# Hymba decode step with PEER retrieval on one core: tiles 4+5, 6+7 and 8+sample share one pass over w_out and w_query

## The reference

```python
h = rmsnorm(x, g_mix) ; c_q, c_kv, k_r, r_q, r_k, r_v, r_g = split(h @ w_in)   # (1024, 2464)
lat = mla_attend(...)                 # 8 heads, latent width 128, causal
ro  = retention(...)                  # 8 heads of 64x64 state, chunks of 128, a scan
x = x + concat(lat @ w_uv, head_norm(ro) * silu(r_g)) @ w_out      # w_out (1024, 1024)
h = rmsnorm(x, g_ffn)
q = h @ w_query                       # w_query (1024, 1024)
for each token and each of 8 heads:   # product keys: 2 x 128 scores, top 16 of each,
    e, gate = top 16 of the pair sums # then top 16 of their sums -> 16 experts
x = x + sum over 128 experts of gate * gelu(u_experts[e] . h) * v_experts[e]
y = rmsnorm(x, g_final)
```

## Time and profile before

| | |
|---|---|
| median of three runs | 3395.66 us (3386.74 to 3405.19) |
| the profiled execution | 3404.81 us, its span 3403.0 us |
| granted TensorE clock | 0.946 of full speed |
| DMA | 1298.59 MB, mean 382 GB/s |
| busy share of TensorE, VectorE, ScalarE, POOL | 86%, 68%, 46%, 38% |

### The profile page before, as it was taken

How to read it: one execution, slowest core, us unless ns; L and a number is a source line. 1 busy time by engine, 2 the same in 40 slices (tenths; PEclk the granted TensorE clock), 3 DMA queues, 4 the chain that set the end, 5 groups by cost and what they waited for, 6 DMA issues and landing times.

```text
span 3403.0 us, 32496 instructions
## 1 busy us (share of the span) xinstructions
PE 2916.1 (86%) x9486; PEld 1498.2 (44%) x9486; DVE 2321.7 (68%) x5531; ACT 1550.6 (46%) x4211; POOL 1300.5 (38%) x1097
## 2 busy tenths in 40 slices
PE   7989899988889898989899878987898888787777
PEld 5755555543445444544444333533353344443222
DVE  1268738785687658774788578866876587677854
ACT  2147334554356344643456345644563455333333
POOL 0023324443344433343445434443444434343432
PEclk8998999999999999999999999999999999899899
DMA  4289999999999999999999999999999999799998
GB/s 173 90 318 362 385 384 405 392 406 418 417 392 388 422 422 408 392 399 417 421 396 414 422 421 422 405 421 422 400 373 418 422 353 330 299 373 421 372 422 346
DMA packets 238361, 1298.59 MB, mean 382 GB/s; under 512 B 45748, under 2 KB 70228, under 8 KB 95462
## 3 DMA queue, kind: packets, MB, share of 16 engines
q0 software_dynamic: 156672, 1140.92, 82.3%
q1 hardware_dynamic: 81510, 155.59, 12.2%
HBM read 1279.41 MB, written 16.44 MB: 381 GB/s over the span
## 4 chain that ended last, share of the span: by engine, by line
PE 44%; DMA 27%; DVE 21%; ACT 4%; issue 2%; POOL 0%; SPq 0%; DVEq 0%; ACTq 0%; POOLq 0%
PE PS L1080 21%; DMA R<-in_t_uv,idx 19%; DVE R L1728 8%; PE PS L763 8%; DMA R<-in_t_uv,idxS 4%; DMA wring<-in_w_out 2%; PE PS L844 2%; PE PS L1002 2%; PE PS L729 2%; PE PS L843 2%; DVE SC L1689 2%; DVE SC L1686 2%; DVE ef L1691 2%; DMA wring<-in_w_query 2%; PE PS L1029 2%
## 5 line engine op out<-in xcount | busy, mean ns | idle before, releaser
L1080 PE MATMUL PS<-R,diag 128*128 128x512 f32 x3616 | 1788.4, 630 | 295.8 <-ACT diag L1355 262.8
L694 POOL DMA_INDIRECT R<-in_t_uv,idx x1024 | 1236.6, 1208 | 1981.1 <-PE PS L1080 1236.6
L1728 DVE CUSTOM_DVE_ANT_0 R<-R,hb 128x1024 f32<-128x1024 f32 x1088 | 1316.3, 1219 | 663.0 <-DMA R<-in_t_uv,idx 581.8
L1080 PEld LDWEIGHTS PS<-R,diag 128*128 128x128 f32 x3616 | 672.1, 198 | 1172.3 <-issue 606.9
L1346 ACT ACTIVATE acts<-dots 128x1 f32<-128x1 f32 x1088 | 217.8, 200 | 1258.8 <-DVE dots L1728 1256.2
L1355 ACT ACTIVATE diag<-ident,wv 128x128 f32<-128x128 f32 x840 | 337.7, 402 | 46.3 <-PE PS L1080 19.3
L763 PE MATMUL PS<-R 128*128 128x256 f32 (+1 forms) x1280 | 296.1, 388 | 42.6 <-ACT stg L1123 36.4
L1348 ACT ACTIVATE wv<-gate,acts 128x1 f32<-128x1 f32 x1024 | 302.0, 295 | 33.2
L763 PEld LDWEIGHTS PS<-R 128*128 128x128 f32 x1280 | 245.9, 199 | 111.8 <-issue 80.2
L1739 DVE SCALAR_TENSOR_TENSOR xb<-R,wv,xb 128x1024 f32<-128x1024 f32 x184 | 235.7, 1281 | 9.5 <-ACT wv L1348 9.5
L1466 DVE CUSTOM_DVE_ANT_0 PP<-PS,mask 128x144 f32<-128x144 f32 (+7 forms) x64 | 49.4, 771 | 170.8 <-PE PS L844 170.7
(11 more groups left out here) (242 smaller groups left out, 2389.9 us busy)
## 6 DMA issues: line engine op xcount, KB each, us to landing
wring<-in_w_out SPq DMA_DIRECT2D x64, 512.0 KB, 12.0
wring<-in_w_query SPq DMA_DIRECT2D x64, 512.0 KB, 8.3
R<-in_t_win SPq DMA_DIRECT2D x27, 1024.0 KB, 12.0
R<-in_t_uv,idx POOLq DMA_INDIRECT x1024, 12.6
pr<-prd SPq DMA_DIRECT2D x8, 976.0 KB, 11.2
prd<-stg SPq DMA_DIRECT2D x54, 128.0 KB, 7.6
xb<-in_x_prompt SPq DMA_DIRECT2D x8, 512.0 KB, 8.5
R<-in_w_out SPq DMA_DIRECT2D x8, 512.0 KB, 4.7
```

The source lines that it names most:

```text
L694: e.indirect_dma_start(dst, None, table, bass.IndirectOffsetOnAxis(ap=index, axis=0)).then_inc(S[s], c.count(name, s, 16))
L1080: m = mm(bank(n), diag[:, NTH[s] % DR, :], pair(s)[:, D + 512 * n:D + 512 * n + 512], start=begins, stop=s == last_slot(t), skip_group_che ...
L1728: e.tensor_tensor_reduce(u, u, hb[:, tile_of(g) % 2, :], 1.0, 0.0, ALU.mult, ALU.add, dots[:, g % NW:g % NW + 1]).then_inc(dve_done, c.cou ...
```

## The change

Tiles 4 and 5, 6 and 7, 8 and 9 become pairs (`PAIRED`), a first tile a and a second tile b. One pass over w_out and one over w_query serves both: `pout`, `pnorm` and `pquery` (34 parts, 48 turns) take the place of two tails, and each block in the ring is used by four matmuls (`pair_rows`, banks 2, 3 for a and 5, 6 for b). The ring of such a pass has two buffers; the third (`spare`) holds a's concatenated heads, then b's normalised input, then b's transposed queries. b's residual x2 lives in `pr`; x2 and h of b are stored to DRAM (`kept`) and loaded into `xb` and `hb` when b's turn comes. b's scores are made later (`scb`). The attention of b, and before it `kv` and `q`, stand ahead of the pair's pass. The sample's loads, attention and retention stand 128 turns earlier. The third pass of `items` ends at turn 464, not 540. The ring of gathers is wide for slots 472 to 671 instead of 550 to 775. Tiles 1 to 3 keep tails of their own, with fewer turns for tile 3.

```diff
@@ -40,7 +40,8 @@
 NR = AUX + 7
 DR = 4
 NW = 16
-WIDE = 4 * P + 38, 6 * P + 8
+WIDE = 3 * P + 88, 5 * P + 32
+PAIRED = {4: 5, 6: 7, 8: SMP}
+    both = lambda a: stage("pout", a) + stage("pnorm", a) + stage("pquery", a)
+    for n, at, end in ((1, 8, 160), (2, 182, 3 * P + 80)):
         spread(stage("ldx", n), at, at + 1)
         spread(prep(n), at + 8, at + 22)
         spread(stage("ldw", n), at + 22, at + 23)
         spread(stage("items", n), at + 26, end)
-    for t in range(1, NTILE):
-        at = P * (t - 1)
-        if t > 1:
-            spread(top(t, 1), at, at + 40)
-        spread(stage("att", t + 1) + stage("ret", t + 1), at + (3 if t > 1 else 17), at + (52 if t > 1 else 58))
-        spread(stage("ldb", t + 1), at + 36 if t > 1 else 8, at + 37)
-        spread(tail(t + 1), at + (52 if t > 1 else 58), at + 96)
-        spread(top(t + 1, 0), at + 96, at + 119)
-        if t + 2 <= NTILE:
-            spread(stage("lda", t + 2), at + 56, at + 57)
-            spread(stage("kv", t + 2) + stage("q", t + 2), at + 100, at + 128)
-    at = P * (NTILE - 2)
-    spread(stage("ldc", SMP), at + 18, at + 52)
-    spread(stage("lds", SMP), at + 54, at + 60)
-    spread(stage("kv", SMP) + stage("q", SMP), at + 97, at + 108)
-    spread(stage("atts", SMP) + stage("rets", SMP), at + 108, at + 180)
-    at += P
-    spread(top(NTILE, 1), at, at + 40)
-    spread(tail(SMP), at + 52, at + 82)
-    spread(top(SMP, 0) + top(SMP, 1), at + 82, at + 118)
-    spread(stage("sts", SMP), at + 84, at + 116)
+    for t in range(2, NTILE + 1):
+        spread(top(t, 1), P * (t - 1), P * (t - 1) + 40)
+    spread(stage("att", 2) + stage("ret", 2), 17, 58)
+    spread(stage("ldb", 2), 8, 9)
+    spread(tail(2), 58, 96)
+    spread(top(2, 0), 96, 119)
+    spread(stage("lda", 3), 56, 57)
+    spread(stage("kv", 3) + stage("q", 3), 100, 126)
+    spread(stage("att", 3) + stage("ret", 3), P + 3, P + 48)
+    spread(stage("ldb", 3), P + 34, P + 35)
+    spread(tail(3), P + 48, P + 86)
+    spread(top(3, 0), P + 92, P + 118)
+    spread(stage("lda", 4), P + 52, P + 53)
+    spread(stage("ldb", 4), P + 60, P + 61)
+    spread(stage("kv", 4) + stage("q", 4), P + 86, P + 98)
+    spread(stage("att", 4) + stage("ret", 4), P + 98, 2 * P + 8)
+    spread(stage("lda", 5) + stage("ldb", 5), 2 * P + 8, 2 * P + 10)
+    spread(stage("kv", 5) + stage("q", 5), 2 * P + 10, 2 * P + 18)
+    spread(stage("att", 5) + stage("ret", 5), 2 * P + 18, 2 * P + 52)
+    for a in PAIRED:
+        at = P * (a - 3)
+        if a > 4:
+            spread(stage("scb", a - 1), at + 41, at + 43)
+            spread(stage("att", a) + stage("ret", a), at + 43, at + (100 if a < NTILE else 94))
+            spread(stage("ldb", a), at + 84, at + 85)
+            spread(top(a - 1, 0), at + 94, at + 119)
+            if a < NTILE:
+                spread(stage("lda", a + 1) + stage("ldb", a + 1), at + 100, at + 102)
+                spread(stage("kv", a + 1) + stage("q", a + 1), at + 108, at + 128)
+                spread(stage("att", a + 1) + stage("ret", a + 1), at + P + 3, at + P + 50)
+        spread(both(a), at + P + 52, at + P + 100)
+        spread(top(a, 0), at + P + 100, at + P + 120)
+        if a < NTILE:
+            spread(stage("lda", a + 2), at + P + 102, at + P + 103)
+            spread(stage("kv", a + 2) + stage("q", a + 2), at + P + 108, at + P + 128)
+    at = P * (NTILE - 3)
+    spread(stage("ldc", SMP), at + 48, at + 82)
+    spread(stage("lds", SMP), at + 94, at + 98)
+    spread(stage("kv", SMP) + stage("q", SMP), at + 100, at + 110)
+    spread(stage("atts", SMP) + stage("rets", SMP), at + 110, at + 180)
+    spread(stage("sts", SMP), at + P + 58, at + P + 90)
+    at = P * (NTILE - 1)
+    spread(stage("scb", SMP), at + 41, at + 43)
+    spread(top(SMP, 0) + top(SMP, 1), at + 43, at + 118)
...
-        gfin = wring[:, 2, :]
+        gfin = wring[:, 0, :]
+        spare = wring[:, 2, :]
+        xpr, tpr = pr[:, 0:D], pr[:, D:2 * D]
+
+        def cat_of(t):
+            return spare if t in PAIRED else hb[:, (t + 1) % 2 if is_b(t) else t % 2, :]
+
+        def kept_of(t, what):
+            row = P * (2 * (t - 1) + what)
+            return kept[row:row + P, :]
+
+        def before(t):
+            return t - 3 if is_b(t) else t - 2
...
-            return 4 if t == 1 else 3
+            return 4 if t == 1 else 2 if t in PAIRED else 3
 
         def w_buf(t, m):
-            return R[:, m % 4, :] if t == 1 else wring[:, m % 3, :]
+            return R[:, m % 4, :] if t == 1 else wring[:, m % w_bufs(t), :]
...
-                e.wait_ge(dve_done, c.at("dve", f"ret{t - 1}"))
+                if is_b(t - 1):
+                    e.wait_ge(pe_done, c.at("pe", f"qqT{t - 1}"))
+                else:
+                    e.wait_ge(dve_done, c.at("dve", f"ret{t - 1}"))
...
+            def load_gfin(t):
+                e.wait_ge(pe_done, c.at("pe", f"used q{t}_{NCH - 1}"))
                 dma(gfin, A["g_final"].partition_broadcast(P), "gfin", f"g{t}")
+
+            def pout(p, a):
+                b = PAIRED[a]
+                yield from p.to(0)
+                for m in range(2):
+                    load_w(a, m, p)
+                e.wait_ge(dve_done, c.at("dve", f"s sn{DEC_B - 1}" if b == SMP else f"ret{b}"))
+                if b == SMP:
+                    x = A["x_sample"].rearrange("b t d -> (b t) d")
+                    dma(xpr[0:NSMP, :], x, "xp", f"a{b}")
+                    dma(xpr[NSMP:P, :], x, "xp", f"x{b}")
+                else:
+                    dma(xpr, x_rows[P * (b - 1):P * b, :], "xp", f"x{b}")
+                for m in range(2, NCH + 2):
+                    yield from p.to(5 + m - 2)
+                    load_w(a, m, p)
+
+            def pnorm(p, a):
+                b = PAIRED[a]
+                yield from p.to(0)
+                e.wait_ge(dve_done, c.at("dve", f"res{b}"))
+                dma(kept_of(b, 0), xpr, "x2st", f"x{b}")
+                yield from p.to(2)
+                e.wait_ge(dve_done, c.at("dve", f"hp{b}"))
+                dma(kept_of(b, 1), spare, "hst", f"h{b}")
+
+            def pquery(p, a):
+                for m in range(NCH + 2, 2 * NCH):
+                    yield from p.to(1 + m - 2 - NCH)
+                    load_w(a, m, p)
+                yield from p.to(8)
+                load_gfin(a)
...
-                if t == SMP:
-                    dma(xb[0:NSMP, t % 2, :], A["x_sample"].rearrange("b t d -> (b t) d"), f"xb{t % 2}", f"a{t}")
-                    dma(xb[NSMP:P, t % 2, :], A["x_sample"].rearrange("b t d -> (b t) d"), f"xb{t % 2}", f"x{t}")
+                if is_b(t):
+                    e.wait_ge(S["x2st"], c.at("x2st", f"x{t}"))
+                    dma(xb[:, t % 2, :], kept_of(t, 0), f"xb{t % 2}", f"x{t}")
+                    e.wait_ge(S["hst"], c.at("hst", f"h{t}"))
+                    dma(hb[:, t % 2, :], kept_of(t, 1), "hbl", f"h{t}")
...
+                for k in range(NCH):
+                    yield from p.to(4 + k)
+                    if k == 0:
+                        e.wait_ge(act_done, c.at("act", f"catT{b}"))
+                    pair_rows(a, k, k, "o")
+
+            def pair_rows(a, m, k, which):
+                e.wait_ge(S[f"w{m % 2}"], c.at(f"w{m % 2}", f"{which}{a}_{k}"))
+                w = w_buf(a, m)
+                for lhs, at in ((T1, 2), (tpr, 5)):
+                    for n in range(2):
+                        i = mm(bank(at + n), lhs[:, P * k:P * k + P], w[:, 512 * n:512 * n + 512],
+                               start=k == 0, stop=k == NCH - 1)
+                i.then_inc(pe_done, c.count(f"used {which}{a}_{k}"))
...
+            def pquery(p, a):
+                b = PAIRED[a]
+                for k in range(NCH):
+                    yield from p.to(k)
+                    if k == 0:
+                        e.wait_ge(act_done, c.at("act", f"hT{b}"))
+                    pair_rows(a, k + NCH, k, "q")
+                yield from p.to(9)
+                e.wait_ge(act_done, c.at("act", f"qq{b}"))
+                transposes(lambda k: scr[:, P * k:P * k + P], H,
+                           lambda k: two(5)[:, P * k:P * k + P]).then_inc(pe_done, c.count(f"qqT{a}"))
+                yield from p.to(11)
+                e.wait_ge(act_done, c.at("act", f"qqT{a}"))
+                scores(a, B1)
+                yield from p.to(13)
+                e.wait_ge(act_done, c.at("act", f"sc{a}"))
+                transposes(lambda k: xpr[:, P * k:P * k + P], H,
+                           lambda k: two(5)[:, P * k:P * k + P]).then_inc(pe_done, c.count(f"qqT{b}"))
+
+            def scb(p, b):
+                yield from p.to(0)
+                e.wait_ge(act_done, c.at("act", f"qqT{b}"))
+                if b < SMP:
+                    e.wait_ge(act_done, c.at("act", f"qlat{b + 1}"))
+                scores(b, spare)
```

187 lines of the change are left out of this document (145 added, 42 removed).

## The result

The changed kernel takes 3441.65 us (median of 4 runs, 3434.39 to 3446.47) against 3392.51 us for the kernel before (4 runs, 3386.74 to 3405.19). The ratio on record is 1.0123 [1.0098, 1.0148]: it is slower, by some 42 us.

The account below looks back on a forecast made before the run. Bytes set the time nearly everywhere, TensorE and chains between engines limiting attention. Terms -49 +60 +5 +18 -5 -5 gave +24 us on 3404.8 us, 3429 us, or 3420 us on the medians' scale; range 3360 to 3475 us.

Parts of the forecast that it names:

- The bytes: Whole kernel: net 20.5 MB less to move, entered as -49 us wherever the DMA is full.
- The main term: Slots 226 to 356: 412 us of matmul take 457 us against 388 us of bytes, 10 absorbed; +60 us.
- absorption: Slots 226 to 356: the gather ring of 8 buffers takes up about 10 us of slower consumption.
- packing share: Slots 226 to 356: how full TensorE can be, 0.89 in the first 82 slots, 0.95 in the pair's 48.
- The ring of two: Pairs' tails: two weight buffers lose 21 us per pair unabsorbed; entered as +5 us second pair, +18 us third.
- the short ring: Rival, 12%: slow weight loads cost 32 us more per pair, 3516 us; sign: waits of 2 us or more per block.
- Stretches after the pairs: After each pair slots should run at 2.5 us each; slots 868 to 1014 at a DMA share of 1.0.
- The sample's attention: Moved 128 slots earlier beside a list search, it keeps its length in slots and costs the same: 0.
- The rival that the bytes decide: Rival, 25% with its neighbourhood: gather ring absorbs every TensorE wait; 3342 to 3371 us, slots 226 to 356 under 395 us.
- Balance: Rival, 22%: TensorE packs at 0.95 and the third pair's loss is partly absorbed; -15 us, 3390 us.

Follow-up runs that it names:

- Experiment 1: Kernel before, loading half the columns of each w_out and w_query block from tile 4 on: 3354.14 us, ratio 0.987.
- x3_half_items: Changed kernel with every second row block left out of the input projection's third pass: 3425.05 us, ratio 1.0077.
- z4_after_dve: Changed kernel with 19 more slots in 226 to 259 and 316 to 355 summed by VectorE instead of TensorE: 3430.1 us, ratio 1.0082.
- y1_att8_dense: Kernel before with the attention and retention of tile 8 in 34 slots instead of 49: 3411.17 us, ratio 1.005.
- y3_pairs45_67: Changed kernel without its third pair, tile 8 and the sample tailed apart and their stages where they stood before: 3442.29 us, ratio 1.0133.

## Why the prediction was right, and where it was off

**The bytes.** "Net 20.5 MB less" was exact: 20.45 MB. Their worth, "-49 us, wherever the DMA is full", was mis-sized. Experiment 1 gives 36 us (27 to 45) for as many, and its tails by the traces 40. Why a MB gives back less than its rate is not shown: the tails of before stand at a DMA share of 1.01 to 1.02. This is the term of the sum that the runs correct. With -36 in its place the sum is +37 us, and the runs' difference is 42. That they come so close is partly luck, as neither is known to better than some 10 us.

**The main term.** "+60 us" for slots 226 to 356. The stretch took 437 us where I had 457, or 447 after absorption, with TensorE busy 410.2 us (my sum was 412 us) and 155.0 MB (mine 157.5):

```profile
911.00:1348.00 437.00, 202.35 (x426) 77.16 (x424) 0.98 0.91 355
...
911.00:1348.00 437.00, 57.91 (x248) 47.96 (x249) 0.98 0.91 355
...
DMA packets 25440, 155.00 MB, mean 355 GB/s; under 512 B 3105, under 2 KB 5285, under 8 KB 8357
```

The first of these rows is the value matmuls alone (mine 204 us), the second the items of the input projection (mine 49 us). Packing was 0.94 over the whole stretch, better than my 0.90 (412 of 457 us). As a loss beyond the bytes, which is how the +60 was defined, it is 437 less 155.0 MB at 406 GB/s (382 us), 55 us before anything that the ring absorbs; the slot times cannot show whether the 10 us of absorption were there. The term was right within some 10 us, and what it gave too much, the stretches behind it gave back too little (-14 where I had -24), which fits bytes worth less.

**What sets the pace there.** The prediction spoke of TensorE's sum over a packing share. The runs show that over 130 slots this is only part. Taking 17 and 24 us from TensorE (x3_half_items, z4_after_dve) shortened the stretch by 7 us each time. One reason is that the sum binds in shorter pieces: in the dense attention of y1_att8_dense, which cost 17 us, TensorE is busy 112.8 of 116 us, and z4_after_dve relieved a pass that was then near the time of its bytes. The other is a cost that TensorE's sum does not hold: smaller lumps returned 13 us and the third buffer 14 us with the same matmuls. A likely link is order: each engine takes its parts in a fixed order, and with fewer slots between a head's parts VectorE and ScalarE stand before its mask and exponent while the slots' own work is queued behind. That chain is in the timeline of one head; that it accounts for the rest in numbers is argued, not shown.

**The ring of two.** "21 us are lost per pair where nothing absorbs them", entered as 5 and 18: a third buffer returned 14 us in all, and in the third pair ring, lumps and density together gave back the bytes' gain (y3_pairs45_67). The pass of the second pair took 146 us and that of the third 161, where I had 150 (145 and 5) and 166. The mechanism was right, and so was the order of the pairs. The sign was not: TensorE's waits per block were to be 1 us or less, and were 0.5, 1.0 and 1.9 us. The last is near the 2 us that I had named as the sign of the short ring. The rival's time is refuted all the same: it would have made the third pass some 198 us, and the third buffer returned 14 ± 12 us, not 48 to 96. What I had set against it, that loads land sooner with fewer gathers in flight, the traces do not show: before, w_out landed after 16.9 us in the tail of tile 8, where gathers took 15.6, and after 13.7 us in that of tile 7, where they took 23.4.

**Stretches after the pairs.** "2.5 us per slot" was met behind the third pair only: slots 940 to 1014 took 186 us, 2.51 a slot, at 419 GB/s. Behind the first it was 2.7 (slots 356 to 387) and behind the second 2.6 (612 to 683). Slots 868 to 1014 stood at a DMA share of 1.01, as said. The sample's attention keeps its length (249 us for 70 slots, before 258 for 72), as "0" said.

**The rival that the bytes decide** needed slots 226 to 356 under 395 us; they took 437. **Balance** needed 0.95 and the third pair absorbed. Its packing was nearly right (0.94); its time of 3390 us was not. The Trainium skill's rule (Perfetto Trace Analysis, Identifying the Most-Contended Engine), to optimise the most-contended engine first, named the DMA over the whole span (94.5% busy, 382 GB/s). The bytes it points to are worth 36 us, but the way to save them overfilled TensorE in the stretches where that was nearly the most-contended one already.

**What stays open.** How much of the packed stretch's cost is TensorE's sum in its short pieces and how much the in-order waits: no kernel here reorders parts within an attention at the same density. Whether the other place of the wide ring (slots 472 to 671 instead of 550 to 775) costs anything: no kernel moves it alone. Whether the single effects add up: 14, 13, 19 and 24 us are each from one order of trying, and each is known to about 10 us. And the 12 us or more by which the runs differ beyond the two traces.

## What to carry to other kernels

A saving of bytes in a kernel whose DMA is full is worth its rate only if the plan that saves them fills no other engine. Sum every engine over the shortest stretch that the change squeezes, since a stretch that overruns isn't repaid by stretches that already run at the DMA's rate. When such a change comes out slower, test the timing before giving it up: here a third buffer, halved lumps, ten slots moved and idle VectorE turned 1.0123 into 0.9916 with the same bytes moved.
